# The gate phase of a PEER decoder kernel: first-layer tiles as three products of high and low parts, and two of eight gated one-hots moved to ScalarE

## What is computed

```
scores of 128 + 128 half keys per head -> 16 best pairs (i1, i2), gates by softmax
y(row) = sum over (head, pair) of gate * gelu(x . u[i1*128 + i2]) * v[i1*128 + i2]
```

## Time and profile before

| | |
|---|---|
| median of 3 runs | 1314.94 us |
| the profiled execution's own time | 1312.16 us |
| its span in the profile | 1310.3 us |
| granted TensorE clock over the span | 0.995 of full speed |
| TensorE busy | 1264.3 us (96%) |
| VectorE busy | 974.5 us (74%) |
| ScalarE busy | 575.5 us (44%) |
| GpSimd busy | 307.4 us (23%) |

### The profile page before, as it was taken

The page is one execution under the profiler, slowest core; times in us unless marked ns, Lnnn a source line. Parts: engine busy times, 40 slices in busy tenths (PEclk is TensorE's granted clock), DMA queues, the critical chain, the costliest instruction groups (busy, mean ns, idle before and its releaser), DMA issues.

```text
span 1310.3 us, 25938 instructions
## 1 busy us (share of the span) xinstructions
PE 1264.3 (96%) x8436; PEld 1075.5 (82%) x8436; DVE 974.5 (74%) x2220; ACT 575.5 (44%) x1067; POOL 307.4 (23%) x521
## 2 busy tenths in 40 slices
PE   9999999889899999999999999999999999999996
PEld 6889888855556678799988988988988988998985
DVE  3666566266604799999988788788788888888886
ACT  4644666254411211143345445445445445545553
POOL 0003230400004588501112122112122222222201
PEclk9999999999999999999999999999999999999998
DMA  8655764579959697759859999999998998998962
GB/s 288 225 163 168 249 224 175 178 279 401 402 211 361 243 334 261 245 192 282 246 177 328 317 321 310 310 323 308 308 327 301 326 318 304 322 318 303 318 193 93
DMA packets 164384, 358.80 MB, mean 274 GB/s; under 512 B 49234, under 2 KB 99090, under 8 KB 160594
## 3 DMA queue, kind: packets, MB, share of 16 engines
q1 hardware_dynamic: 133410, 241.46, 54.5%
q0 software_dynamic: 25424, 111.37, 24.1%
q10 hardware_dynamic: 5472, 4.98, 1.2%
HBM read 341.56 MB, written 53.35 MB: 301 GB/s over the span
## 4 chain that ended last, share of the span: by engine, by line
PE 50%; DVE 4%; issue 2%; DVEq 1%; ACT 1%; POOLq 0%; POOL 0%; ACTq 0%
PE psum L1932 26%; PE psum L1921 7%; PE psum L1920 7%; PE psum L1919 7%; PE psum L1437 2%; PE psum L1945 2%; DVE gated_i L2080 2%; DVE v_lo L2093 0%; DVEq L2080 0%; ACT v_hi L2001 0%; DVE OT L2076 0%; DVE ln_bn L1364 0%; DVE x L1358 0%; DVE gated_lo L2129 0%; DVE x L1387 0%
## 5 line engine op out<-in xcount | busy, mean ns | idle before, releaser
L1921 PE MATMUL psum<-x_hi,u_lo 128*128 128x256 f32 x760 | 215.1, 283 | 0.0
L1920 PE MATMUL psum<-x_lo,u_hi 128*128 128x256 f32 x760 | 215.0, 283 | 0.0
L1919 PE MATMUL psum<-x_hi,u_hi 128*128 128x256 f32 x760 | 214.6, 282 | 0.0
L2093 DVE TENSOR_TENSOR v_lo<-big,v_hi 128x1024 fp32r<-128x1024 f32 x128 | 156.8, 1225 | 35.1 <-ACT v_hi L2001 34.6
L2001 ACT ACTIVATE v_hi<-big 128x1024 fp32r<-128x1024 f32 x128 | 135.4, 1057 | 83.4 <-PE psum L1932 81.2
L1932 PE MATMUL psum<-v_hi,gated_hi 128*128 128x512 f32 x512 | 159.9, 393 | 1.0 <-DVE gated_lo L2129 1.0
L1932 PE MATMUL psum<-v_lo,gated_hi 128*128 128x512 f32 x512 | 158.7, 390 | 0.0
L1932 PE MATMUL psum<-v_hi,gated_lo 128*128 128x512 f32 x512 | 158.3, 390 | 0.0
L1919 PEld LDWEIGHTS psum<-x_hi,u_hi 128*128 128x128 f32 x760 | 145.5, 191 | 3.7
L1920 PEld LDWEIGHTS psum<-x_lo,u_hi 128*128 128x128 f32 x760 | 145.5, 191 | 3.7
L1921 PEld LDWEIGHTS psum<-x_hi,u_lo 128*128 128x128 f32 x760 | 145.5, 191 | 0.0
(11 more groups left out here) (325 smaller groups left out, 2508.7 us busy)
## 6 DMA issues: line engine op xcount, KB each, us to landing
big<-in_peer_v SPq DMA_DIRECT2D x128, 512.0 KB
big<-in_peer_u SPq DMA_DIRECT2D x115, 512.0 KB, 5.0
w_then_a_vals<-in_a_v SPq DMA_DIRECT2D x8, 2048.0 KB
keep_ak<-in_a_k POOLq DMA_DIRECT2D x32, 508.0 KB, 6.5
keep_av<-in_a_v POOLq DMA_DIRECT2D x24, 512.0 KB, 6.3
big<-in_a_k SPq DMA_DIRECT2D x4, 2048.0 KB, 10.3
a_keys<-in_a_k SPq DMA_DIRECT2D x4, 2048.0 KB, 12.4
wq_ring<-in_peer_wq SPq DMA_DIRECT2D x16, 512.0 KB, 6.5
```

The lines of the kernel that those rows point to most:

```text
L1919: pe.matmul(H[:, 0:SEQ], uh[:, q, kc], x1h[:, k, :], start=(k == 0), stop=False)
L1920: pe.matmul(H[:, 0:SEQ], uh[:, q, kc], x1l[:, k, :], start=False, stop=False)
L1921: mm = pe.matmul(H[:, 0:SEQ], ul[:, q, kc], x1h[:, k, :], start=False, stop=(k == KD - 1))
L2093: ve.tensor_tensor(vl[:, q], vs[:, q], vh[:, q].bitcast(F32), ALU.subtract).then_inc(s["v_lo"], 1)
```

## The change

1. Early tiles 19 to 31 (`SPLIT = EARLY_R + 4` = 19) are computed as 24 fp32r products of 256 columns instead of 8 fp32 ones. ScalarE makes the high part (`early_hi`, into the new tile `uph`), GpSimd subtracts for the low part (`early_lo`, into `upl`, which lies over `up`).
2. VectorE writes 6 of the 8 gated one-hots of a step. ScalarE writes two (`gated`), as relu(gate - gate*|i1 - iota|), with two activations each. It does so two steps ahead, in front of the phase for steps 0 and 1, and behind `W_out(c)` for step c+2.
3. `uph` lies over columns 2048 to 4095 of `big`. So the loads of v tiles 0 and 1 move on SyncE's queue behind the stores of W and the first loads of W tiles, and wait for early tiles 30 and 31.
4. The negated gates `ngt` are one more VectorE instruction at the end of the routing stage.
5. Some semaphores move from one list to the other, by which they are allocated later.

```diff
@@ route_block, vector
             after(ve.tensor_copy(t.gt[:], gT[:]))
+            after(ve.tensor_scalar(t.ngt[:], gT[:], -1.0, None, ALU.mult))
@@ expert_block, sync
-            for m in range(2):
-                sp.wait_ge(s["hp_mm"], EARLY_R + m + 4)
-                sp.dma_start(vs[:, m], d.peer_v[m]).then_inc(s[f"ld_v2{m}"], 16)
...
             for p in range(2):
                 load_w(p, p)
+            for m in range(2):
+                sp.wait_ge(s["hp_mm"], EARLY - 1 + m)
+                sp.dma_start(vs[:, m], d.peer_v[m]).then_inc(s[f"ld_v2{m}"], 16)
@@ expert_block, tensor: gate_rows, early
                 pe.wait_ge(s["onehot"], c + 1)
+                pe.wait_ge(s["onehot_act"], c + 1)
...
-                    pe.wait_ge(s[f"ld_e{n % 2}"], 16 * ((n - EARLY_R - 4) // 2 + 1))
-                    early_hidden(pe, t, s, n, up[:, n % 2])
+                    pe.wait_ge(s["hp_lo"], n - SPLIT + 1)
+                    pe.wait_ge(s["hp_out"], n - 1)
+                    out = bank(5 + 2 * (n % 2))[:, 0:SEQ]
+                    for k in range(KD):
+                        kc = slice(k * P, (k + 1) * P)
+                        pe.matmul(out, t.uph[:, n % 2, kc], x1h[:, k, :], start=(k == 0), stop=False)
+                        pe.matmul(out, t.uph[:, n % 2, kc], x1l[:, k, :], start=False, stop=False)
+                        mm = pe.matmul(out, upl[:, n % 2, kc], x1h[:, k, :], start=False, stop=(k == KD - 1))
+                    mm.then_inc(s["hp_mm"], 1)
@@ expert_block, scalar
+            def early_hi(n):
+                act.wait_ge(s[f"ld_e{n % 2}"], 16 * ((n - SPLIT) // 2 + 1))
+                act.wait_ge(s["hp_mm"], max(n - 1, SPLIT))
+                act.activation(t.uph[:, n % 2], up[:, n % 2], ACT.Copy).then_inc(s["hp_hi"], 1)
+            def gated(c, q):
+                if c >= 2:
+                    act.wait_ge(s["c_mm"], c + 1)
+                for x in range(BY_ACT):
+                    r = c * GT + GT - BY_ACT + x
+                    ins = act.activation(dist[:, q, x], iof, ACT.Abs, bias=t.i1[:, r:r + 1], scale=-1.0)
+                ins.then_inc(s["act_dist"], 1)
+                act.wait_ge(s["act_dist"], c + 1)
+                for x in range(BY_ACT):
+                    r = c * GT + GT - BY_ACT + x
+                    ins = act.activation(A[:, q, GT - BY_ACT + x], dist[:, q, x], ACT.Relu, bias=t.gt[:, r:r + 1], scale=t.ngt[:, r:r + 1])
+                ins.then_inc(s["onehot_act"], 1)
+            act.wait_ge(s["iota_in"], 16)
+            for c in range(2):
+                gated(c, c)
             for n in (EARLY_R - 1, EARLY_R):
                 early_out(act, d, t, s, n)
...
                     if c % 2 == 0:
+                        if SPLIT <= EARLY_R + 2 + c // 2 < EARLY:
+                            early_hi(EARLY_R + 2 + c // 2)
                         early_out(act, d, t, s, EARLY_R + 1 + c // 2)
                     W_out(c, g, GT * (c % STEPS), c % 2)
+                    if c + 2 < GROUPS * STEPS:
+                        gated(c + 2, c % 2)
@@ expert_block, vector
-                for r in range(GT):
+                for r in range(GT - BY_ACT):
@@ expert_block, gpsimd
+            def early_lo(n):
+                gp.wait_ge(s["hp_hi"], n - SPLIT + 1)
+                gp.tensor_tensor(upl[:, n % 2], up[:, n % 2], t.uph[:, n % 2].bitcast(F32), ALU.subtract).then_inc(s["hp_lo"], 1)
+            for n in range(SPLIT, EARLY):
+                if n >= SPLIT + 2:
                     gp.wait_ge(s["hp_mm"], n - 1)
                 gp.dma_start(up[:, n % 2], d.peer_u[4 * early_place(n)]).then_inc(s[f"ld_e{n % 2}"], 16)
+                if n == SPLIT + 1:
                     for m in range(UN):
                         gather_u(m)
+                if n >= SPLIT + 1:
+                    early_lo(n - 1)
+                if n >= SPLIT + 2 and n % 2 == 0:
+                    m = UN + (n - SPLIT - 2) // 2
                     gp.wait_ge(s["dots"], m - UN + 1)
                     gather_u(m)
+            early_lo(EARLY - 1)
```

More of the change, by code:

```diff
@@ L1787 @@
 GRP = 64
+BY_ACT = 2
 HWC = TILES * P
@@ L1813, in expert_block @@
             A = only.enter_context(nc.sbuf_tensor("gated_i1", [P, 2, GT, P], F32))
+            with ExitStack() as place:
+                upl = place.enter_context(nc.sbuf_tensor("early_u_lo", [P, 2, D], F32R))
             up = only.enter_context(nc.sbuf_tensor("early_u", [P, 2, D], F32))
@@ L1819, in expert_block @@
         E = t.OT[:].rearrange("p k n -> p (k n)")[:, 0:2 * GT * NE].rearrange("p (s r j) -> p s r j", s=2, r=GT)
+        dist = t.OT[:].rearrange("p k n -> p (k n)")[:, 2 * GT * NE:2 * GT * NE + 2 * BY_ACT * P].rearrange("p (s r j) -> p s r j", s=2, r=BY_ACT)
         iof = t.big[:, BIG_IOTA:BIG_IOTA + P]
@@ L1841, in expert_block @@
         DOTS0, FIRST = 8, 7
+        SPLIT = EARLY_R + 4
         def plain(k):
@@ L2180, in gather_v @@
                   .then_inc(s[f"ld_g{m % UN}"], 16)
-            for n in range(EARLY_R + 4, EARLY):
-                if n >= EARLY_R + 6:
+            def early_lo(n):
[3 more added lines that the diff above has]
+                if n >= SPLIT + 2:
                     gp.wait_ge(s["hp_mm"], n - 1)
                 gp.dma_start(up[:, n % 2], d.peer_u[4 * early_place(n)]).then_inc(s[f"ld_e{n % 2}"], 16)
-                if n == EARLY_R + 5:
+                if n == SPLIT + 1:
                     for m in range(UN):
                         gather_u(m)
-                if n >= EARLY_R + 6 and n % 2 == 0:
-                    m = UN + (n - EARLY_R - 6) // 2
+                if n >= SPLIT + 1:
+                    early_lo(n - 1)
+                if n >= SPLIT + 2 and n % 2 == 0:
+                    m = UN + (n - SPLIT - 2) // 2
                     gp.wait_ge(s["dots"], m - UN + 1)
                     gather_u(m)
+            early_lo(EARLY - 1)
             for m in range(m + 1, 64):
@@ L2293 @@
 ld_wq3 ln_sum ln_st ln_mean ln_var ln_root ln_fac ln_scaled ln_lg
-ln_l ln_rg ln_r top topr topb top2 ixf be ber beb bei pr128 pair pair_v bf g_sub g_exp g_den g_fin id_eq id_mul id_sum
+ln_l ln_rg ln_r bei pr128 pair pair_v bf g_sub g_exp g_den g_fin id_eq id_mul id_sum
 id_turn id_out split y_done ld_u0 ld_u1 ld_v20 ld_v21 ld_ln2 y_low u_hi u_lo v_hi v_lo h_mm gelu hw hw_hi hw_lo y_mm c_mm
-W_out onehot zero iota_in st_y""".split()
-LATE_SEMS = """o_mm x_turn x_out x_hi x_lo q_mm q_out sc_mm sc_out x1_twice ld_g0 ld_g1 ld_g2 ld_g3 dots dots_kept n_gelu values st_w0 st_w1 ld_w0 ld_w1
-ld_p0 ld_p1 ld_p2 ld_p3 ld_e0 ld_e1 hp_mm hp_out st_h0 st_h1 ld_h0 ld_h1 gelu_p""".split()
+W_out zero iota_in st_y""".split()
+LATE_SEMS = """onehot onehot_act act_dist top topr topb top2 ixf be ber beb o_mm x_turn x_out x_hi x_lo q_mm q_out sc_mm sc_out x1_twice ld_g0 ld_g1 ld_g2 ld_g3 dots dots_kept n_gelu values st_w0 st_w1 ld_w0 ld_w1
+ld_p0 ld_p1 ld_p2 ld_p3 ld_e0 ld_e1 hp_mm hp_hi hp_lo hp_out st_h0 st_h1 ld_h0 ld_h1 gelu_p""".split()
 def build(nc, d, upto=9):
@@ L2310, in build @@
             t.w1h = place.enter_context(nc.sbuf_tensor("w1_hi", [P, 2, 4096], F32R))
+        with ExitStack() as place:
+            place.enter_context(nc.sbuf_tensor("big_us", [P, 2 * D], F32))
+            t.uph = place.enter_context(nc.sbuf_tensor("early_u_hi", [P, 2, D], F32R))
         t.big = sb("big", [P, KD * D])
@@ L2376, in build @@
         t.sg = sb("sample_gates", [P, 64])
+        t.ngt = sb("gates_negated", [P, SEQ])
         route_block(nc, d, t, s)
```

## The result

The changed kernel takes 1333.7 us (median of 4) against 1314.7 (median of 4) measured with it: ratio 1.0145, 95% interval 1.0132 to 1.0158. It is slower, as forecast, but by 19.0 us and not by 10.4; 1333.7 lies 0.7 us above the upper end of the range. The profiled execution of the changed kernel took 1332.9 us, with a span of 1331.1. Measured again with the last experiment it took 1330.7 us, ratio 1.0121 (1.0103 to 1.0140), so a difference between two versions that were not measured together is good to 2 or 3 us only.

What follows compares the result with a forecast made beforehand. VectorE, held by GpSimd's early_lo, was taken to bound the gate phase at 8.18 us per pair: +9.9 us, with small edits +10.4, so 1322.6 profiled and 1325.3 us median; range 1309 to 1333.

Steps and rivals of the forecast that it cites:

- the mechanism that decides: Gate phase: VectorE and GpSimd take turns, so each early_lo costs VectorE 2.25 us, 29.2 us over 13.
- TensorE's tile: Gate phase: a first-layer tile in fp32r costs 2.87 us against 3.46, saving 7.7 us over 13 tiles.
- VectorE's step: Gate phase: two gated one-hots fewer make a VectorE step 2.68 us instead of 3.19.
- The rival without turns: Gate phase: VectorE runs on beside early_lo, so the kernel gets faster, 1305.5 to 1308.4 us; chance 0.11.
- The landings: Gate phase: waits of early_hi for loads of `up`, 0 to 0.9 us a tile, taken as 0 with +5 for the range.
- the v loads: SyncE's queue: v loads moved behind W stores and two W loads, priced at 0, at most +3 us.
- the main loop unchanged: Main loop: 5.62 us from one group of products to the next, as before.
- Half turns: Gate phase: only VectorE's two-input instructions wait for early_lo, 15.6 us lost in all; 1311.7, up to 1316 us; chance 0.12.
- the quick form that L896 shows: VectorE: A has L896's form, where doubling 128 columns adds 61 ns; taken as sign that A waits too.
- the sum of the phase: Gate phase from step 5 at 568.4: 81.5 of VectorE work, 29.2 of early_lo, 1.95 last gate_rows; end 681.1, +9.9 us.
- The start: Start of gate phase: two `gated` before early_out(14) hold ScalarE 3.1 us and early(16) waits for that output: +0.2 us.
- the rival in which ScalarE is late: Gate phase: late landings stall early_hi and W_out on top of the turns, 13 x 0.9 us more, 1337 us; chance 0.06.

Runs made afterwards that it cites:

- e1: The changed kernel with GpSimd's subtraction cut from 1024 columns to 8, the third product taking the high part of u: 1308.2 us, ratio 0.9960 to before.
- e3: The kernel before with eleven GpSimd subtractions of 768 columns added in the gate phase, results never read: 1334.2 us, ratio 1.0169 to before.
- e9: The kernel before with eleven GpSimd memsets of 768 columns added at the places of e3's subtractions: 1319.2 us, ratio 1.0032 to before.
- e5: The changed kernel without `gated`: VectorE writes all eight gated one-hots, split products and GpSimd's subtraction stay: 1343.3 us, ratio 1.0213 to before.
- e12: The changed kernel as it is, measured again beside e11: 1330.7 us, ratio 1.0121 to before.
- e11: The changed kernel with zero matmuls ahead of seven TensorE waits and tile 14's eviction and store before the first `gated`: 1327.0 us, ratio 1.0095 to before.

## Why the prediction was half right

**Right.** The sign, and the mechanism that decides: GpSimd's subtraction takes VectorE's time, E's and A's alike (e1, e3). TensorE's tile: 24 products 0.12 us apart are 2.87 us, as worked out. VectorE's step: 585.92 to 588.59 is 2.67 in the same timeline, 2.68 said. ScalarE: one `gated` behind another 1.50 us later (552.16 to 553.66), 1.5 said, and e1's 6.70 per pair stands for the 6.54. The rival without turns was given 1305.5 to 1308.4 us; e1, which is that case, took 1308.2. The landings at 0, the v loads at 0 and the main loop unchanged hold nearly: `early_hi` waited for its load once, 1.3 us, and TensorE twice for `early_lo`, 1.7 us. Half turns would have been about 1312; A waits (e3), and the reason given for it, the quick form that L896 shows, fits e9, where A is held even by an operation that only writes.

**The term that was too high.** `early_lo` took 2.43 us, not 2.26, but each cost VectorE 1.80, not 2.25: E and A take 114.7 us here and 91.3 in e1, 23.4 over 13. Where it starts while VectorE waits for TensorE, a part is free. That is 5.8 us less than the sum had; in e3 and e5, where VectorE waits less, the loss per microsecond is higher (0.96 and 0.81 against 0.74; e5: 133.5 - 108.2 = 25.3 for 31.1 us).

**The step that failed** is the sum of the phase with VectorE full from step 5 on: "TensorE's 7.7 us turn into waiting", and no term for VectorE's own waits for TensorE. The runs showed 12.2 us of such waits in its place (9.1 in e12). The reading that seemed to confirm the sum was wrong already: the 4.5 us that close it for the kernel before are not all behind step 5, 2.0 of them are ahead of it (VectorE's timeline before), and that it closed within 0.4 us was luck.

```profile
559.23 1.23 DVE L2076 TENSOR_TENSOR OT<-big,i 128x1024 f32<-128x1024 f32 x1 [2.04 <-PE psum L1945]
```

With its own numbers, and what the trace has for each:

| from step 5 to the last W_out, us | predicted | after |
|---|---|---|
| start of step 5 (568.10 + 2.67) | 568.4 | 570.8 |
| 27 steps, 6 dots, 2 u_lo (the same prices) | 81.5 | 81.5 |
| holds | 29.2 | 23.4 |
| VectorE's waits for TensorE (16.4 less those at 560.58, 3.31, and at 568.10, 0.94) | 0 | 12.2 |
| last gate_rows (one predicted; the last two ran back to back, from 688.45) | 1.95 | 3.7 |
| not placed | | 0.6 |
| end | 681.1 | 692.2 |

The holds are uneven: one step of VectorE takes 2.67 us and the next 4.8, while a pair's work of TensorE is 6.44. There are only two buffers of one-hots. So when VectorE is held, TensorE runs dry for 2.5 us; then TensorE's part comes late, at 1.2 GHz for a while, and now VectorE has no free buffer and waits up to 2.65 us. Each engine's lateness is handed to the other, and a mean of 8.18 against 6.44 per pair does not show that. I read the clock in no row, because the kernel before has 1.00 throughout; the trace after has it, and e11 puts its share at about 4 us. Counted from step 5 on, as in the table, VectorE waits 9.1 us for TensorE in e12 and still 5.6 in e11, where the clock is mended. I put what stays down to the unevenness; no run tests that by itself, and a third one-hot buffer was not tried.

**The start** was sized at +0.2 us. The row of the trace has 6.84 us of waiting for a store, and the first W_out comes 4.2 us later than before, of which 1.2 are the block's own later start (551.35 against 550.15) and 3.0 the two `gated` and that store (1.6 in e12). Of it the medians with the store first show nothing that is clear of their scatter.

**The range.** Its upper end came from 2.4 us per hold and from the rival in which ScalarE is late. Both terms that were missed lie on the slow side, and neither had a bound in it.

## What to carry to other kernels

An idle engine is not free room if its instructions hold the full one: price a move to GpSimd by its whole duration, taken from VectorE, before anything else (of a subtraction's duration 0.74 to 0.96 was lost here). Here the same subtraction costs 1.8 us from VectorE when it runs on GpSimd and 1.13 when VectorE does it itself, so the idle engine is the dearer one. And where two engines near their bounds pass work through two buffers, an uneven delay on one is paid on both; sum the steps in order, not their mean.

## What was not expected of the hardware

- A GpSimd memset of 768 columns, which reads nothing, itself takes 0.76 us and costs VectorE 0.83 to 0.96 when A's of one input stand beside it, and nothing beside the dot of two inputs (1.23 us as always).
- The granted clock fell not in TensorE's wait of 2.56 us but after work had begun again, and was back at 1.00 while the work went on: it was 0.50 from about 586.3 (worked out from the mean of 0.80 between 584.9 and 587.2) to about 589.6.
- A wait alone does not settle whether the clock falls. In e3 TensorE waited 2.43 us at 593.06 and the 16 matmuls behind it took 3.68 us, and behind a wait of 2.49 at 667.75 they took 3.33; after waits of 2.34 us (611.35) and 2.48 us (649.59) the same 16 took 2.05. What tells them apart no run shows.
